# One step of a recurrent, sliding-window and mixture-of-experts layer on one core: a different order of mixer steps, loads and ring places, a reordered tail, and low parts of weights split inside the wait for the tanh

## What is computed

```
u = x @ w_in + b_in           # columns: lru_x | lru_y | q | k | v | gate_lru | gate_attn
xc = causal depthwise conv of width 4 over lru_x
r, i = sigmoid(xc @ w_rg + b_rg), sigmoid(xc @ w_ig + b_ig)    # 16 diagonal blocks of 64 x 64
log_a = -8 * r * softplus(-lru_lambda)
h = scan(exp(log_a), sqrt(1 - exp(2 * log_a)) * (i * xc))
rec = h * gelu(lru_y)                                          # gelu with tanh
att = window attention (128 keys, 16 heads, 4 kv heads, sinks); samples attend to cache_k, cache_v
mix = (sigmoid(gate_lru) * (rec @ w_lru_out) + sigmoid(gate_attn) * (att @ w_attn_out)) @ w_o
x1 = LayerNorm(alpha * x + mix)
y = LayerNorm(alpha * x1 + experts(x1))     # top 1 of 4 groups, then top 2 of its 8 experts
expert e: (silu(x @ w_gate[e]) * (x @ w_up[e])) @ w_down[e]    # 32 experts, 6 MB each
```

## Time and profile before

| | us |
|---|---|
| median of 3 runs | 1030.9 |
| lowest and highest | 1029.38 and 1034.28 |
| the profiled execution | 1030.14 |
| its span (first to last instruction) | 1028.3 |
| TensorE busy in the span | 886.4 (86%) |
| VectorE busy | 447.9 (44%) |
| ScalarE busy | 280.7 (27%) |
| GpSimd busy | 117.6 (11%) |
| moved by DMA | 263.16 MB, 256 GB/s over the span |

### The profile page before, as it was taken

How to read it: one execution, slowest core, us unless ns; L and a number is a source line. 1 busy time by engine, 2 the same in 40 slices (tenths; PEclk the granted TensorE clock), 3 DMA queues, 4 the chain that set the end, 5 groups by cost and what they waited for, 6 DMA issues and landing times.

```text
span 1028.3 us, 14537 instructions
## 1 busy us (share of the span) xinstructions
PE 886.4 (86%) x5897; PEld 615.0 (60%) x5897; DVE 447.9 (44%) x922; ACT 280.7 (27%) x537; POOL 117.6 (11%) x202
## 2 busy tenths in 40 slices
PE   6899999899999999999749999997777877777870
PEld 6789999789899989998733333332332322322330
DVE  3865876774555645442462232332212212222207
ACT  3667544345344422211311111111010110110113
POOL 2000300000000010030130122211111111111110
PEclk9999999989999999999959999999999999999995
DMA  9324621212122232439389999999999999999946
GB/s 285 113 62 82 189 78 63 81 42 83 48 77 82 51 81 85 121 137 415 145 332 419 423 421 422 424 420 423 425 420 423 424 422 422 423 421 423 422 174 232
DMA packets 85957, 263.16 MB, mean 256 GB/s; under 512 B 28767, under 2 KB 59643, under 8 KB 65250
## 3 DMA queue, kind: packets, MB, share of 16 engines
q1 hardware_dynamic: 78850, 246.94, 61.9%
q0 software_dynamic: 7040, 15.28, 4.0%
HBM read 257.36 MB, written 15.16 MB: 265 GB/s over the span
## 4 chain that ended last, share of the span: by engine, by line
PE 43%; SPq 27%; DMA 13%; DVE 10%; ACT 3%; issue 3%; POOL 1%; POOLq 0%; DVEq 0%; ACTq 0%
PE ps L768 28%; SPq L506 22%; PE ps L1065 5%; SPq L509 4%; PE ps L1092 4%; DMA slot<-in_w_up 3%; DMA xg<-x_half,idG 3%; DMA ff_half<-xg,idD 2%; DMA raw<-in_w_o 2%; DMA raw<-in_w_in 1%; PE ps L894 1%; PE ps L884 1%; DVE rawL L1418 1%; PE ps L860 1%; DVE hL L1499 1%
## 5 line engine op out<-in xcount | busy, mean ns | idle before, releaser
L1065 PE MATMUL ps<-slot,xt 128*64 128x512 f32 x512 | 231.9, 600 | 47.6 <-DMA slot<-in_w_up 46.8
L1066 PE MATMUL ps<-slot,xt 128*64 128x512 f32 x512 | 232.4, 601 | 0.0
L1065 PEld LDWEIGHTS ps<-slot,xt 128*64 128x64 f32 x512 | 66.4, 137 | 184.4 <-issue 139.7
L768 PE MATMUL ps<-xTh,wh 128*128 128x260 f32 x704 | 147.0, 290 | 4.0 <-DVE rawL L1418 4.0
L768 PE MATMUL ps<-xTl,wh 128*128 128x260 f32 x704 | 143.1, 285 | 0.0
L768 PE MATMUL ps<-xTh,rawL 128*128 128x260 f32 x704 | 143.1, 285 | 0.0
L1092 PE MATMUL ps<-slot,hT 128*64 128x512 f32 x512 | 116.9, 597 | 19.1 <-issue 17.7
L1418 DVE TENSOR_TENSOR rawL<-raw,wh 128x1024 fp32r<-128x1024 f32 x68 | 84.1, 1240 | 81.7 <-ACT wh L1150 81.6
L768 PEld LDWEIGHTS ps<-xTh,wh 128*128 128x128 f32 x704 | 110.0, 192 | 9.9 <-issue 9.1
L768 PEld LDWEIGHTS ps<-xTl,wh 128*128 128x128 f32 x704 | 110.2, 191 | 0.0
L768 PEld LDWEIGHTS ps<-xTh,rawL 128*128 128x128 f32 x704 | 109.9, 191 | 0.0
(11 more groups left out here) (316 smaller groups left out, 1243.0 us busy)
## 6 DMA issues: line engine op xcount, KB each, us to landing
slot<-in_w_gate SPq DMA_DIRECT2D x64, 1024.0 KB, 30.5
slot<-in_w_up SPq DMA_DIRECT2D x64, 1024.0 KB, 31.5
slot<-in_w_down SPq DMA_DIRECT2D x31, 2048.0 KB, 33.0
raw<-in_w_in SPq DMA_DIRECT2D x18, 1024.0 KB, 5.2
raw<-in_w_in SPq DMA_DIRECT2D x16, 256.0 KB, 4.4
raw<-in_w_lru_out SPq DMA_DIRECT2D x4, 1024.0 KB, 4.8
raw<-in_w_attn_out SPq DMA_DIRECT2D x16, 256.0 KB, 4.5
raw<-in_w_o SPq DMA_DIRECT2D x4, 1024.0 KB, 5.2
```

The source lines that it names most:

```text
L768: last = mm(out_of[:, a, 0:HT], w[:, k, :], x[:, k, a * HT:(a + 1) * HT], start=(k == 0 and n == 0), stop=(k == KT - 1 and n == 2))
L1065: mm(out[0:CAP, :], tokens, w[:, q, :], start=start, stop=stop)
L1066: last = mm(out[CAP:P, :], tokens, w[:, 4 + q, :], start=start, stop=stop)
```

## The change

- **Start.** The second weight chunk is issued right behind the first, ahead of the vectors. The two clears of the gates' weight buffers are dropped (the numbers of the counter s_cst fall by two). GpSimd's two copies of the key and value cache to the outputs wait until four tiles are done. Tile 0 is made by `first_passes`: 16 products of high by high, 16 with the low part of x, 16 with the low part of the weights, each group waiting only for what it reads. VectorE makes the low parts of tiles 0 to 3 before the loop, ScalarE takes lru_lambda's exponential after reading tile 0, and the logarithm's polynomial has 8 instructions in place of 15.
- **ly tiles.** VectorE makes the low part of tile t+3 between the polynomial and the wait for the tanh, not ahead of the tile. The samples' attention steps stand earlier in the table: cache transposes after tiles 18 and 19 (in banks 4 and 5), scores after 21, exponentials as a step of their own (`sx`) after 22, then `sn` 23, `st` 24, `sp` 25.
- **Attention product.** The first ao tile is made by `attended_passes`: the half with tokens 0 to 259 waits only for seven of eight units, the other half for the last and for the samples.
- **Loads.** The last chunk of w_o is issued behind load 0. Load 8 waits for the logits only, load 9 for the stores of x1, load 10 for the tables. Slots 9 and 10 have changed places, and router temporaries and the experts' small buffers have other addresses. Three of four `xg` buffers are cleared ahead of the stores of x1, one after them.
- **Tail.** ScalarE does a Sqrt on one column after its last norm copy. `finish(0)` stands ahead of `summed(1)`. The last block's last instruction and its store come in two halves of 512 columns.

```diff
+_place(20, ("oh",))
...
-_place(20, ("oh",))
-_place(21, ("sk", 0))
-_place(22, ("sk", 1))
-_place(23, ("ss",))
-_place(24, ("sn",))
-_place(25, ("st",))
-_place(26, ("sp",))
+_place(18, ("sk", 0))
+_place(19, ("sk", 1))
+_place(21, ("ss",))
+_place(22, ("sx",))
+_place(23, ("sn",))
+_place(24, ("st",))
+_place(25, ("sp",))
...
+        slot = [at(f"slot{n}", [P, 8, 512], F32, SLOT * (n if n < 9 else 19 - n)) for n in range(RING)]
...
             half_chunk(0)
+            half_chunk(1)
...
-            half_chunk(1)
-
-            sp.wait_ge(s_cst, 2)
...
-            for hc in range(2, NT // 2):
+            for hc in range(2, NT // 2 - 1):
                 half_chunk(hc)
...
                 if hc == 32:
                     sp.wait_ge(s_zx, 8)
                     load(0)
+                    half_chunk(hc + 1)
                     load(1)
                     sp.wait_ge(s_mg, 8)
                     load(2)
@@ -538,12 +541,13 @@
             load(7)
             sp.wait_ge(s_zt, 4)
             sp.wait_ge(s_lg, 1)
+            load(8)
             sp.wait_ge(s_x1o, 16 * TT)
-            load(8)
+            sp.wait_ge(s_oh10, 2)
+            load(9)
             sp.wait_ge(s_tabc, 4)
             for n, name in enumerate(("ln2_g", "ln2_b")):
                 sp.dma_start(vec32[n * KT:(n + 1) * KT, :], A[name].rearrange("(k n) -> k n", n=P)).then_inc(s_l2, 16)
-            load(9)
             load(10)
...
-                sp.dma_start(dst, f0[n][0:ROWS[n], :]).then_inc(s_yo, 16)
-            sp.wait_ge(s_yo, 16 * TT)
+                if m < TT - 1:
+                    sp.dma_start(dst, f0[n][0:ROWS[n], :]).then_inc(s_yo, 16)
+                else:
+                    sp.dma_start(dst[:, 0:512], f0[n][:, 0:512]).then_inc(s_yo, 16)
+                    sp.wait_ge(s_y2, TT + 1)
+                    sp.dma_start(dst[:, 512:D], f0[n][:, 512:D]).then_inc(s_yo, 16)
+            sp.wait_ge(s_yo, 16 * (TT + 1))
...
-            gp.memset(wrg[:, :, :], 0.0).then_inc(s_cst, 1)
-            gp.memset(wig[:, :, :], 0.0).then_inc(s_cst, 1)
...
+            pool.wait_ge(s_proj, 4)
             pool.dma_start(O["k_win_sample"][:, 0:WIN - 1, :, :].rearrange("b w k d -> b (w k d)"),
                            A["cache_k"][:, 1:WIN, :, :].rearrange("b w k d -> b (w k d)")).then_inc(s_kv_out, 16)
...
+            for j in range(NXG - 1):
+                link(gp.memset(xg[j][:, :], 0.0))
             for m, n in enumerate(ORDER):
                 pool.wait_ge(s_x1, m + 1)
                 pool.dma_start(x1_rows[n * P:n * P + ROWS[n], :].rearrange("t (c n) -> t c n", c=4),
                                zn[m][P - ROWS[n]:P, :, :]).then_inc(s_x1o, 16)
             pool.wait_ge(s_x1o, 16 * TT)
-            for j in range(NXG):
-                link(gp.memset(xg[j][:, :], 0.0))
+            link(gp.memset(xg[NXG - 1][:, :], 0.0))
             pool.wait_ge(s_tabc, 1)
...
+            def first_passes(out_of, hi, lo, rhs_h, rhs_l):
+
+                for n, (w, x) in enumerate(((hi, rhs_h), (hi, rhs_l), (lo, rhs_h))):
+                    if n == 1:
+                        pe.wait_ge(s_xl, TT)
+                    if n == 2:
+                        pe.wait_ge(s_lo, 1)
+                    for k in range(KT):
+                        for a in range(2):
+                            last = mm(out_of[:, a, 0:HT], w[:, k, :], x[:, k, a * HT:(a + 1) * HT],
+                                      start=(k == 0 and n == 0), stop=(k == KT - 1 and n == 2))
+                return last
...
+            def attended_passes(out_of, hi, lo, rhs_h, rhs_l):
+
+                for a in range(2):
+                    if a == 1:
+                        pe.wait_ge(s_attl, NUNIT)
+                        pe.wait_ge(s_sal, 2)
+                        pe.wait_ge(s_sah, 2)
+                    for k in range(KT):
+                        for n, (w, x) in enumerate(((hi, rhs_h), (hi, rhs_l), (lo, rhs_h))):
+                            last = mm(out_of[:, a, 0:HT], w[:, k, :], x[:, k, a * HT:(a + 1) * HT],
+                                      start=(k == 0 and n == 0), stop=(k == KT - 1 and n == 2))
+                return last
...
             def tile(t):
                 kind, i = TILES[t]
                 rhs_h, rhs_l = {"lo": (recH, recL), "ao": (attH, attL), "wo": (mgH, mgL)}.get(kind, (xTh, xTl))
                 if t == 0:
-                    pe.wait_ge(s_xl, TT)
+                    pe.wait_ge(s_xh, TT)
                 if kind == "lo" and i == 0:
                     pe.wait_ge(s_rec, 8)
                 if kind == "ao" and i == 0:
-                    pe.wait_ge(s_attl, NUNIT)
-                    pe.wait_ge(s_sal, 2)
-                    pe.wait_ge(s_sah, 2)
+                    pe.wait_ge(s_attl, NUNIT - 1)
                 pe.wait_ge(s_hi, t + 1)
+                if t == 0:
+                    first_passes(pair[0], wh[0], wcol(0, rawL), rhs_h, rhs_l).then_inc(s_proj, 1)
+                    return
                 pe.wait_ge(s_lo, t + 1)
                 if t >= 2:
                     pe.wait_ge(*emptied(t - 2))
+                if kind == "ao" and i == 0:
+                    attended_passes(pair[t % 2], wh[t % (AHEAD + 1)], wcol(t, rawL), rhs_h, rhs_l).then_inc(s_proj, 1)
+                    return
                 passes(pair[t % 2], wh[t % (AHEAD + 1)], wcol(t, rawL), rhs_h, rhs_l,
                        kind == "wo" and i == 0).then_inc(s_proj, 1)
...
                 pe.wait_ge(s_h, 16)
-                pe.wait_ge(s_ttr, 8)
+                pe.wait_ge(s_ska, 2)
+                pe.wait_ge(s_skd, 2)
...
                     pe.wait_ge(s_ck, 16)
-                    pe.wait_ge(s_attl, 1)
-                    pe.wait_ge(s_pd, 2)
+                    pe.wait_ge(s_ttr, 8)
...
+                pe.wait_ge(s_attl, 1)
...
-            act.wait_ge(s_lam, 1)
-            sc.activation(lam[:, 1, :], lam[:, 0, :], ACT.Exp, scale=-1.0).then_inc(s_lamE, 1)
...
+                    if t == 0:
+                        act.wait_ge(s_lam, 1)
+                        sc.activation(lam[:, 1, :], lam[:, 0, :], ACT.Exp, scale=-1.0).then_inc(s_lamE, 1)
...
-                elif what == "ss":
+                elif what == "sx":
                     sample_exps()
...
+            sc.activation(nb[:, 0:1], epsT[:, 1:2], ACT.Sqrt)
...
-            for t in range(2):
+            for t in range(AHEAD + 1):
                 w_lo(t)
...
-                for n in (13, 11, 9, 7, 5, 3, 1):
-                    link(v.tensor_tensor(p_, p_, q_, ALU.mult))
-                    link(v.tensor_scalar(p_, p_, 1.0 / n, None, ALU.add))
-                link(v.tensor_tensor(p_, p_, s_, ALU.mult))
+                link(v.tensor_tensor(p_, p_, q_, ALU.mult))
+                for n in (13, 11, 9, 7, 5, 3):
+                    link(v.scalar_tensor_tensor(out=p_, in0=p_, scalar=1.0 / n, in1=q_, op0=ALU.add, op1=ALU.mult))
+                link(v.scalar_tensor_tensor(out=p_, in0=p_, scalar=1.0, in1=s_, op0=ALU.add, op1=ALU.mult))
...
                     v.tensor_tensor(y2[:, :], y2[:, :], yb[:, :], ALU.mult).then_inc(s_yq, 1)
+                    w_lo(t + AHEAD)
                     dve.wait_ge(s_yt, i + 1)
...
-            for t in range(2, AHEAD):
-                w_lo(t)
             for step in STEPS:
                 what, args = step[0], step[1:]
                 if what == "tile":
                     t = args[0]
-                    if t + AHEAD < NT:
+                    kind, i = TILES[t]
+                    if 0 < t < NT - AHEAD and kind != "ly":
                         w_lo(t + AHEAD)
...
-                v.scalar_tensor_tensor(out=z[0:r, :], in0=zc[m % 2][0:r, :], scalar=mv[0:r, m, 3:4], in1=ln2B[0:r, :],
-                                       op0=ALU.mult, op1=ALU.add).then_inc(s_y2, 1)
+                for c in range(2 if m == TT - 1 else 1):
+                    part = slice(c * 512, (c + 1) * 512) if m == TT - 1 else slice(0, D)
+                    v.scalar_tensor_tensor(out=z[0:r, part], in0=zc[m % 2][0:r, part], scalar=mv[0:r, m, 3:4], in1=ln2B[0:r, part],
+                                           op0=ALU.mult, op1=ALU.add).then_inc(s_y2, 1)
 
             summed(0)
-            for m in range(TT):
+            finish(0)
+            summed(1)
+            for m in range(1, TT):
                 if m + 1 < TT:
                     summed(m + 1)
                 finish(m)
```

68 lines of the change are left out of this document (34 added, 34 removed).

## The result

The changed kernel takes 1026.2 us, median of 6 runs (1024.96 to 1028.68), against 1030.95 for the kernel before (6 runs, 1029.38 to 1036.95). The ratio is 0.9941 with a 95% interval of 0.9917 to 0.9965: faster by 0.6%, where 1.2% was forecast, and the time lies 3.2 us above the top of the range. The profiled execution took 1025.9 us with a span of 1024.1, 4.2 less than before.

What follows compares the result with a forecast made beforehand. It took the mixer, the time until the experts' weight stream runs without a gap, the stream and the tail as the bound. Terms 4.6 + 1.5 + 1.4 + 4.1 - 0.4 + 1.3 = 12.5 gave 1018.4 us, range 1010 to 1023.

Steps and rivals of the forecast that it cites:

- What bounds the kernel: Whole kernel: the experts' weight stream sets its stage's pace; before it, the mixer and when the first expert starts count.
- Start: Mixer's first tiles: first product 1.4 us sooner, both gate waits (3.2), blamed on the late second chunk, gone; 4.6 gained.
- The upper bound's condition: Mixer's start: the first products do not run into the lower clock, which cost 1.6 us; bound 6.2.
- ly tiles: Second linear branch: VectorE and ScalarE bind; saved waits less a longer chain gain 1.5 us, bounds -1 and 9.
- Attention product: First attention tile: its split halves let 24 products cover a wait; 1.4 us gained.
- Output product: Output weights' last chunk comes some 10 us sooner, removing a 2.4 us wait and the lower clock; 4.1 gained.
- The mixer's sum: Mixer: the gains of start, second linear branch, attention product and output product together, 11.6 us.
- From mixer to stream: Mixer's end to gapless weight stream: stores 3 us late beside slot 8, fuller ring; -0.4 us, bounds -1.5 and 1.8.
- Tail: Kernel's end: 8-row tile uses VectorE's idle gap, last store in halves; 1.3 us gained, bounds 0.3 and 2.5.
- Rival 3: Mixer: waits only change place, it keeps its length but for 1.4 us at start and 1.4 at attention; 1027, chance 0.06.

Runs made afterwards that it cites:

- e5: e4 with slot 8 issued when the index table's first product is made; 1019.5 us, ratio 0.9875 to the kernel before.
- e1: The changed kernel with the old order of loads (slot 8 behind the stores of x1, 9 and 10 behind the tables); 1022.2 us, ratio 0.988.
- e4: e1 with the tail's early Sqrt moved behind the branch for overflowing experts; 1019.7 us, ratio 0.9869.
- e10: The kernel before with only the second weight chunk issued right behind the first; 1031.2 us.
- e12: The kernel before with the second weight chunk right behind the first and GpSimd's two cache copies behind the fourth tile; 1030.7 us.
- e8: e4 with the last chunk of w_o behind three slots and the first attention product whole again; 1026.2 us, ratio 0.9937.

## Why the prediction was wrong, step by step

- **What bounds the kernel**: right. From the refill on the two kernels ran alike, and "what counts is when the first expert starts" is where the 8.2 us were lost. It has a limit that the prediction did not draw: a refill earlier than 38 us behind the mixer's end won nothing (e5), as slots 9 and 10 were still on their way.
- **Start** (4.6, upper bound 6.2): tile 9 starts at 75.84 instead of 81.95, 6.1 sooner. The upper bound's condition came true in this profile: the clock was 1.00 where it had been 0.56. In e1 and e4, the same program there, it was not: tile 9 at 77.50 and 77.28, 4.5 and 4.7 won. The nine profiles with this start won 3.3 (e5) to 6.1, 4.9 in the mean. So the size was right, but the cause given for the 3.2 us was wrong (e10, e12): not the late chunk but the order of work on ScalarE and VectorE, for which the chunk is only the condition. The late high part at 23.31 was a wait that another one covered.
- **ly tiles** (1.5, bounds -1 and 9): -0.6 in this profile (97.5 to 98.1), +1.0 (e5) to -2.1 (e1) in the others with the same program here. The forecast that waits stay at the sample's transpose and unit 1's transposes was right (2.2, 2.7, 1.5). Adding VectorE's saved waits up into a gain was the weak step, and "VectorE and ScalarE bind, not TensorE" with it: they came back as its waits for the tile, and TensorE's idle time from tile 24 on stayed at 6.4.
- **Attention product** (1.4): 1.5. **Output product** (4.1): 4.3, with the clock at 1.00, as said. e8, with both undone, confirms them in sum.
- **The mixer's sum** (11.6): 11.3, partly by luck. In this profile the start brought 1.5 us more than forecast, which is the clock's, and the ly tiles 2.1 less.
- **From mixer to stream** (-0.4, bounds -1.5 and 1.8): -8.2. This is the step that failed; it is off by 7.8 us, as much as the time. It failed in two places. For slot 8 beside the stores it allowed 3 us; it cost 5.1, about the slot's whole time. The slot's second half was issued at 497.57 and landed 19.1 us later, at 516.7, the last store at 518.9: all of the slot's 2 MB went ahead of the stores' end. In the stretch from 506 to 518 of the changed kernel the queue of the slots took 47.4% of the engines' time and that of the stores 43.5%:

```profile
q1 hardware_dynamic: 321, 2.38, 47.4%
q0 software_dynamic: 573, 2.09, 43.5%
```

  And it took "the same 1.3 from index to gather" and then left the gather's own duration at 4.1, without asking what would move beside it. In the old order slot 8 landed at 532.4, just ahead of the gather's rows, and slot 9 was issued only at 532.29; in the new one 4 MB stood beside the gather, and it took 8.95. The gather's duration stands in neither bound of the term. The Trainium skill (DMA: Bandwidth & Descriptors, section on queues, rings and completion order) says that an engine goes round robin between its queues by packets. The near equal shares of time fit taking turns, but these rows do not show turns of one packet each: 573 packets of the stores went beside 321 of the slots, in about as many bytes. Of the 1.5 us that the prediction drew from that rule: two transfers of 2 MB that take turns evenly end together, when 4 MB are moved, so even turns give nearly all of 5. And by the prediction's own steps stores that land 1.5 late make a term of about +1.2, not the +0.5 stated there.
- **Tail** (1.3, bounds 0.3 and 2.5): 1.1 between the two profiles (32.7 to 31.6 us from the last expert product to the end), but 0.4 between the means given with e4. From the start of VectorE's last instruction (1023.99 before, 1020.25 after) to the end of the span 4.3 us became 3.9, which is the 0.4 forecast for the last store in halves. The three table loads came as said, and the 8-row tile ended at 1005.2, 12.8 behind the last product, where the forecast's 1008.1 less the product's 995.6 is 12.5. The Trainium skill (ScalarE: Activation LUTs, section on table sets) advises grouping; with the Sqrt behind the branch the calls are grouped and one load is left, and 0.6 us is won, not 1.2, since the rows come next.
- **Rivals**: none of the four was this one. Rival 3 had a similar sum for another reason. The missing rival was in the text of the change itself: transfers that are issued earlier than the stores and the gather that the first expert needs.
